# Stationary tiles at the weight ring's 512-byte residue, and two panels whose last units run token tile by token tile

## What is computed

```
x = _layer_norm(DEEPNORM_ALPHA * x + gate1 * y, ln1_g, ln1_b)      # y = merged branches @ w_out
h = x * (1.0 + scale2) + shift2
u = conv3(h @ w_up) + conv_b                                        # 1024 -> 5632, three taps over the tokens
gate, val = split(u);  y = (silu(gate) * val) @ w_down              # 2816 -> 1024
x = _layer_norm(DEEPNORM_ALPHA * x + gate2 * y, ln2_g, ln2_b)       # the output

_layer_norm(x, g, b) = (x - mean(x)) * rsqrt(mean((x - mean(x))**2) + 1e-5) * g + b      # over the 1024 columns
```

## Time and profile before

| | |
|---|---|
| Runs | 1011.33, 1012.34, 1013.93 us; median 1012.34 |
| Profiled execution | 1012.67 us; its span from first to last instruction 1011.1 us |
| Mean granted TensorE clock | 0.985 of 2.4 GHz |
| PE busy | 961.3 us (95%) |
| DVE busy | 747.0 us (74%) |
| ACT busy | 551.7 us (55%) |
| POOL busy | 168.2 us (17%) |
| HBM traffic | 172 GB/s over the span |

### The profile page before, as it was taken

One profiled execution on the slowest core, in us unless ns is written; L12 is line 12 of the kernel. 1 busy time (PEld: TensorE's weight loads), 2 busy tenths in 40 slices (PEclk: granted clock), 3 DMA queues, 4 the chain that ended last, 5 costly groups with the idle time before them and its releaser, 6 DMA issues.

```text
span 1011.1 us, 13813 instructions
## 1 busy us (share of the span) xinstructions
PE 961.3 (95%) x4652; PEld 766.0 (76%) x4652; DVE 747.0 (74%) x1086; ACT 551.7 (55%) x816; POOL 168.2 (17%) x250
## 2 busy tenths in 40 slices
PE   7999999998999899999999999999999699999995
PEld 6787887876767778888888887777777588777884
DVE  5787467876676778886778796756567979999945
ACT  6557646465765455555333436755543367777532
POOL 7000000118100000110111011530000313333400
PEclk9999999998999999999999999999999899999998
DMA  8675443865542347886789564211225255556551
GB/s 259 208 249 156 140 157 123 299 199 172 167 156 88 132 135 243 268 265 213 251 293 316 179 208 148 74 63 50 76 82 189 63 180 168 171 169 215 177 188 41
DMA packets 99746, 175.11 MB, mean 173 GB/s; under 512 B 8252, under 2 KB 36444, under 8 KB 99692
## 3 DMA queue, kind: packets, MB, share of 16 engines
q1 hardware_dynamic: 92460, 148.87, 45.5%
q0 software_dynamic: 7184, 25.50, 7.5%
q10 hardware_dynamic: 48, 0.04, 0.0%
HBM read 173.33 MB, written 1.05 MB: 172 GB/s over the span
## 4 chain that ended last, share of the span: by engine, by line
PE 75%; DVE 13%; ACT 6%; issue 5%; DMA 2%; DVEq 0%; SPq 0%; ACTq 0%
PE acc L706 58%; DVE wlo L1650 3%; PE scores L1108 3%; PE turned L1116 3%; PE turned L758 2%; ACT whi L1233 2%; DVE ltb_lo L1690 1%; DMA raw<-in_w_mem_kv 1%; PE turned L732 1%; DVE turn L1705 1%; PE scores L969 1%; PE scores L902 1%; DVE conv L2385 1%; PE scores L968 1%; DVE turn L1708 1%
## 5 line engine op out<-in xcount | busy, mean ns | idle before, releaser
L1650 DVE TENSOR_TENSOR wlo<-raw,whi 128x1024 fp32r<-128x1024 f32 (+2 forms) x270 | 346.3, 1304 | 111.6 <-ACT whi L1233 103.0
L1233 ACT CAST whi<-raw 128x1024 fp32r<-128x1024 f32 (+2 forms) x270 | 273.5, 1030 | 193.0 <-PE acc L706 148.7
L706 PE MATMUL acc<-whi,lta_lo 128*128 128x512 f32 (+2 forms) x576 | 228.4, 397 | 4.9 <-DVE lta_lo L1690 3.3
L706 PE MATMUL acc<-wlo,lta_hi 128*128 128x512 f32 (+2 forms) x576 | 222.8, 387 | 0.0
L706 PE MATMUL acc<-whi,lta_hi 128*128 128x512 f32 (+2 forms) x576 | 222.5, 386 | 0.0
L706 PEld LDWEIGHTS acc<-whi,lta_lo 128*128 128x128 f32 x576 | 108.6, 189 | 39.5 <-issue 13.5
L706 PEld LDWEIGHTS acc<-wlo,lta_hi 128*128 128x128 f32 x576 | 108.5, 188 | 22.1
L706 PEld LDWEIGHTS acc<-whi,lta_hi 128*128 128x128 f32 x576 | 108.7, 189 | 19.7
L706 PE MATMUL acc<-whi,ltb_lo 128*128 128x512 f32 (+1 forms) x272 | 110.3, 406 | 7.9 <-DVE ltb_lo L1690 4.1
L602 POOL DMA_DIRECT2D wm<-in_w_mod x48 | 34.4, 719 | 466.4 <-DVEq L1750 268.4
L706 PE MATMUL acc<-whi,ltb_hi 128*128 128x512 f32 (+1 forms) x272 | 107.2, 394 | 0.0
(11 more groups left out here) (341 smaller groups left out, 1414.7 us busy)
## 6 DMA issues: line engine op xcount, KB each, us to landing
raw<-in_w_in SPq DMA_DIRECT2D x88, 512.0 KB, 4.1
wm<-in_w_mod POOLq DMA_DIRECT2D x48, 512.0 KB, 5.6
raw<-in_w_up SPq DMA_DIRECT2D x88, 256.0 KB, 3.0
raw<-in_w_up SPq DMA_DIRECT2D x32, 512.0 KB, 4.5
raw<-in_w_down SPq DMA_DIRECT2D x32, 512.0 KB, 4.9
raw<-in_w_down SPq DMA_DIRECT2D x44, 256.0 KB, 3.3
raw<-in_w_mem_kv SPq DMA_DIRECT2D x8, 512.0 KB, 5.8
raw<-in_w_o SPq DMA_DIRECT2D x8, 512.0 KB, 3.4
```

The source lines that it names most:

```text
L706: ins = pe.matmul(acc[s][:, t, 0:n], lhs[part][:, kt0 + kk, tok], w[:, u % RING, kk, 0:n], start=(k == 0 and kk == 0 and j == 0), stop=(la ...
L1233: act.copy(whi[:, s, :, 0:n], raw[:, s, :, 0:n]).then_inc(hi_ready, 1)
L1650: dve.tensor_tensor(wlo[:, s, :, 0:n], raw[:, s, :, 0:n], whi[:, s, :, 0:n].bitcast(F32), ALU.subtract)\
```

## The change

Two parts.

**Addresses.** Tiles are no longer placed by the allocator's scopes but by `Room`, which gives each an address: a multiple of 64 bytes, and, behind `stationary()`, one that is 128 modulo 512. `ckT`, `ltb`, `ff` and `act` (and `arena`, `kvx`, `diag`, the attention's tiles) thus move from 352 to 128 modulo 512, which is what `whi`, `wlo` and `lta` have. `prob`, `probT`, `turn` and `work` move from 160 to 192. `sig` and `tap` take the place behind `ltb`.

**Token order.** `tokens_in_turn` runs the last four units of OUT1 (all it has) and of DN1 (units 7 to 10) first for token tile 0, all four, then for tile 1. The layer norm of tile 0 follows `first_tokens`, that of tile 1 the panel's end. The variance, root, reciprocal and scaling are per tile. ACT's and DVE's splits of UP0.0 to UP0.2 now stand between the two tiles' parts.

```diff
+    LINE, END, TILE, FIRST = 64, 229344, 512, 128
...
+    def stationary(self):
+        return Room(-(-(self.at - self.FIRST) // self.TILE) * self.TILE + self.FIRST)
...
-        one = ExitStack()
+        shared = base.stationary()
+        one = shared.here()
...
-        ltb = [sb(f"ltb_{n}", [P, KT, SEQ], F32R) for n in ("hi", "lo")]
-        kvx = sb("kvx", [P, T, COLS])
-        two = ExitStack()
+        ltb = [sb(f"ltb_{n}", [P, KT, SEQ], F32R, shared) for n in ("hi", "lo")]
+        last = shared.here()
+        kvx = sb("kvx", [P, T, COLS], F32, shared)
+        two = shared.stationary()
...
-                for t in range(T):
+                for t in tokens:
...
-                ins.then_inc(unit_used, 1)
+                if T - 1 in tokens:
+                    ins.then_inc(unit_used, 1)
+                elif last:
+                    ins.then_inc(ev(f"{name}_first_tokens"), 1)
+
+            def tokens_in_turn(name, lhs):
+
+                n = units_of(name)
+                for t in range(T):
+                    for k in range(n - RING, n):
+                        unit(name, k, lhs, tokens=(t,))
...
-            panel("OUT1", lta)
+            tokens_in_turn("OUT1", lta)
...
-            turn_tokens("x3", x, ready="x3_ready")
+            turn_tokens("x3", x, ready="x3_ready", after=2)
...
+            for k in range(FT2 // UNIT - RING):
+                unit("DN1", k, actT)
+            tokens_in_turn("DN1", actT)
...
-            ahead(PLAN.unit["UP0"])
-
-            def variance(name):
+            ahead(PLAN.unit["UP0"] - AHEAD)
+
+            def variance(name, pos):
...
-                sqrt(name, stat[:, 1, 4:6])
-
-            variance("ln1")
+                    act.wait_ge(ev(f"{name}_var"), t + 1)
+                    act.activation(stat[:, 1, 4 + t:5 + t], stat[:, 1, 4 + t:5 + t], ACT.Sqrt).then_inc(ev(f"{name}_std"), 1)
+                    ahead(pos)
+
+            variance("ln1", PLAN.unit["UP0"])
...
+            def layer_norm(gate, name, src, pos, scaled):
+
+                panel_wait(f"{src}0")
...
                 for t in range(T):
-                    ins = dve.tensor_scalar(x[:, t, half], x[:, t, half], stat[:, 1, 2 + t:3 + t], stat[:, 1, 4 + t:5 + t],
-                                            ALU.add, ALU.mult)
-                ins.then_inc(ev("x3_ready"), 1)
+                    residual_sums(gate, src, 0, t)
+                for t in range(T):
+                    if t == 0:
+                        ahead(last_unit(f"{src}1") + 1 - AHEAD)
+                        dve.wait_ge(ev(f"{src}1_first_tokens"), 1)
+                    else:
+                        ahead(pos - 1)
+                        dve.wait_ge(unit_used, RING + last_unit(f"{src}1") + 1)
+                    residual_sums(gate, src, 1, t)
+                    dve.tensor_scalar(stat[:, 1, 2 + t:3 + t], stat[:, 1, 8 + t:9 + t], stat[:, 1, 10 + t:11 + t],
+                                      -1.0 / D, ALU.add, ALU.mult).then_inc(ev(f"{name}_mean"), 1)
+                    dve.wait_ge(ev(f"{name}_mean"), t + 1)
+                    if t == T - 1:
+                        ahead(pos)
+                    scaled(t, lambda: spread_of(name, t))
+
+            def spread_of(name, t):
+
+                v = stat[:, 1, 4 + t:5 + t]
+                dve.wait_ge(ev(f"{name}_sum"), t + 1)
+                var(v, D, LN_EPS).then_inc(ev(f"{name}_var"), 1)
+                dve.wait_ge(ev(f"{name}_std"), t + 1)
+                done(dve.reciprocal(v, v))
+
+            def ln1_scaled(t, spread_known):
+
+                if t == T - 1:
+                    for g in range(2):
+                        b, k = T_USE[f"gate2.{g}"]
+                        dve.wait_ge(t_full[b], k + 1)
+                        dve.tensor_copy(gate_row[:, COLS * g:COLS * g + COLS], tb[b][:]).then_inc(t_free[b], 1)
+                spread_known()
+                for half in (slice(0, COLS), slice(COLS, D)):
+                    dve.tensor_scalar(x[:, t, half], x[:, t, half], stat[:, 1, 2 + t:3 + t], stat[:, 1, 4 + t:5 + t],
+                                      ALU.add, ALU.mult).then_inc(ev("x3_ready"), 1)
...
+            def ln2_scaled(t, spread_known):
+
                 done(dve.scalar_tensor_tensor(work[:, t, :], x[:, t, :], stat[:, 1, 2 + t:3 + t], lnrow[:, 0], ALU.add,
                                               ALU.mult))
-                if t == 0:
-                    layer_norm_var("ln2")
-            inverse("ln2", stat[:, 1, 4:6])
-            for t in range(T):
+                spread_known()
                 dve.scalar_tensor_tensor(x[:, t, :], work[:, t, :], stat[:, 1, 4 + t:5 + t], lnrow[:, 1], ALU.mult, ALU.add)\
                    .then_inc(ev("y_ready"), 1)
```

More of the change, by code:

```diff
@@ L199, with __init__, take, here @@
 LT_ORDER = ["me", "h", "y", "hc", "h2", "x2", "oab", "ym", "x3"]
+class Room:
+    LINE, END, TILE, FIRST = 64, 229344, 512, 128
+    def __init__(self, at):
+        assert at % self.LINE == 0, at
+        self.at = at
+    def take(self, size):
+        self.at += -(-size // self.LINE) * self.LINE
+        assert self.at <= self.END, self.at
+    def here(self):
+        return Room(self.at)
+    def stationary(self):
+        return Room(-(-(self.at - self.FIRST) // self.TILE) * self.TILE + self.FIRST)
 def hybrid_kernel(nc, a, out):
@@ L207, in sem, with sb @@
             return ctx.enter_context(nc.semaphore(name))
-        def sb(name, shape, dt=F32, scope=ctx):
-            return scope.enter_context(nc.sbuf_tensor(name, shape, dt))
+        def sb(name, shape, dt=F32, room=None):
+            room = base if room is None else room
+            v = nc.alloc_sbuf_tensor_at(name, shape, dt, offset=room.at)
+            room.take(int(np.prod(shape[1:])) * (1 if dt is I8 else 4))
+            return v
+        base = Room(16512)
         acc = [ctx.enter_context(nc.psum_tensor(f"acc{i}", [P, T, COLS], F32)) for i in range(2)]
@@ L268, in hybrid_kernel @@
         gmask = sb("gmask", [P, 7, P], I8, one)
-        one.close()
         def ar(at, *shape):
@@ L319, in hybrid_kernel @@
         up = [prob, probT]
-        two.close()
-        diag = sb("diag", [P, KT, P])
-        ones = sb("ones", [P, P])
-        gate_row = sb("gate_row", [P, D])
-        three = ExitStack()
+        later = shared.stationary()
+        diag = sb("diag", [P, KT, P], F32, later)
+        ones = sb("ones", [P, P], F32, later)
+        gate_row = sb("gate_row", [P, D], F32, later)
+        three = later.here()
         qkv = sb("qkv", [P, T, 1536], F32, three)
@@ L331, in hybrid_kernel @@
         ym = work
-        three.close()
-        four = ExitStack()
+        four = later.here()
         lnrow = sb("lnrow", [P, 2, D], F32, four)
@@ L338, in hybrid_kernel @@
         conv = [sb("conv", [P, 4, SEQ], F32, four)[:], work[:, 0].rearrange("p (j s) -> p j s", j=4)]
-        sig = sb("sig", [P, 2, SEQ], F32, four)
-        tap = sb("tap", [P, 4, 4], F32, four)
-        four.close()
+        sig = sb("sig", [P, 2, SEQ], F32, last)
+        tap = sb("tap", [P, 4, 4], F32, last)
         landed = [sem(f"weights_landed{i}") for i in range(RING)]
@@ L690, in _, with unit @@
             pe.sem_inc(unit_used, RING)
-            def unit(name, k, lhs, n=COLS, first_kt=None, i=None, per=0):
+            def unit(name, k, lhs, n=COLS, first_kt=None, i=None, per=0, tokens=range(T)):
                 u, (s, cnt) = PLAN.unit[name] + k, PLAN.bank(name)
@@ L721, in t_begin, with turn_tokens @@
                 return tb[b], t_full[b]
[L723 removed]
+            def turn_tokens(name, src, kts=KT, ready=None, per=2, groups=None, after=0):
                 for g in groups or range(kts // 2):
                     if ready and g % per == 0:
[L727 removed]
+                        pe.wait_ge(ev(ready), after + g // per + 1)
                     bank, full = t_begin(f"{name}.{g}" if kts > 2 else name)
@@ L1209, in _ @@
                             conv_turn(c - 1, i)
-            for c in range(2):
-                for k in range(FT2 // UNIT):
-                    if c == 0 and k == 2:
-                        conv_turn(10)
-                    if c == 0:
-                        pe.wait_ge(conv_mul, k + 1)
-                    unit(f"DN{c}", k, actT)
+            for k in range(FT2 // UNIT):
+                if k == 2:
+                    conv_turn(10)
+                pe.wait_ge(conv_mul, k + 1)
+                unit("DN0", k, actT)
+            for k in range(FT2 // UNIT - RING):
+                unit("DN1", k, actT)
+            tokens_in_turn("DN1", actT)
         def last_unit(name):
@@ L1631, in _ @@
             ahead(PLAN.units)
-            variance("ln2")
+            variance("ln2", PLAN.units)
         @block.vector
@@ L2329, in _, with residual_sums @@
                 lt_dve("ym", lta, groups=(2 * c, 2 * c + 1))
-            def layer_norm_sums(name, src):
+            def residual_sums(gate, src, g, t):
+                part = slice(COLS * g, COLS * g + COLS)
```

(9 more changed lines are left out.)

39 lines of the change are left out of this document (7 added, 32 removed).

## The result

The changed kernel takes 1005.88 us (median of 7 runs, 1001.01 to 1012.32) against 1012.34 (1011.33 to 1013.93): 0.9933 of it, interval 0.991 to 0.9957. It is faster, by 6.5 us (the interval is 4.4 to 9.1) where 7.7 was forecast, inside the range. Its profiled execution took 1008.62 us with a span of 1007.0.

What follows compares the result with a forecast made beforehand. The prediction took PE as 75% of the chain, paying only where PE isn't waiting. It summed -4.85 + 0.4 + 0.45 - 3.73 = -7.7 us against 1012.67, giving 1005.0 us; own range 1002.5 to 1007.8, with rivals 1001.0 to 1009.6.

Steps and rivals of the forecast that it cites:

- The addresses: Matmuls whose stationary tile moves from 352 to 128 modulo 512 get faster, 4.85 us less in all, ends 3.9 and 5.4.
- WD: Its 384 matmuls, all on PE's path, gain 6.1 ns each: 2.3 us less.
- DN and what lies ahead of it: DN's matmuls behind the last convolution, with PE time gained before: 1.65 us less; UP's first part: 0.3 less.
- UP's beat: In UP, DVE, POOL and ACT alone set 12.48 us a panel, so faster matmuls there only lengthen PE's waits: nothing.
- Rival A: The addresses do nothing; slow tiles share being higher in the partition than lta: 1009.8 us, chance 0.12.
- B: UP's pace has a PE step after all, so its ten panels gain 2.8 us: 1002.2 us, chance 0.12.
- C: UP's panels get longer, DVE standing behind one more POOL instruction in each, ten costing 13 us: 1018 us, chance 0.04.
- Token order in OUT1: In OUT1 PE waits 0.3 us for OUT1.3's split and restarts for 0.1: 0.4 us more.
- The first layer norm: Between OUT1 and UP0, splits ahead of tile 1's residual delay the turned x to T + 6.75, T the panel's end: +0.45 us.
- POOL's lock: Behind the first layer norm, POOL's product stretches DVE's subtraction from 0.68 to 4.90 us: neither worse nor better.
- The end: Behind DN1 only one tile's norm remains, 4.98 us where 8.71 was: 3.73 less; second store at most 0.3 less, not counted.
- the clock: A fall to 0.50 of 2.4 GHz for 3.4 us in UP0, behind the layer norm's idle, costs 1.7 us, may come or not.

Runs made afterwards that it cites:

- b1: The changed kernel with ckT, ff, act and ltb at 192 modulo 512, the ring and lta left at 128: 1008.0 us in one execution.
- b2: The changed kernel with everything 224 bytes higher, ring, lta and all other stationary tiles at 352 modulo 512: 1003.35 us in one execution.
- b4: The changed kernel with lta alone moved to 320 modulo 512, all other stationary tiles left at 128: 1011.09 us in one execution.
- e1: The changed kernel with ACT's cast of act_hi in UP behind the next panel's first two weight casts, and ckT 128 bytes on: 1002.81 us.
- e2: Token order with the addresses of before, and ACT's cast of act_hi in UP behind the next panel's first two weight casts: 1008.33 us.
- d2: The changed kernel, POOL's gain and bias behind the last convolution in eight pieces, UP0.1's and UP0.2's splits behind the subtractions, ckT at 320 modulo 512: 995.97 us.
- a2: The token order alone, with the allocator's addresses of before: 1009.32 us against 1012.24 for the kernel before, 0.9974 of it.
- a3: The changed kernel with OUT1 and the first layer norm as before: 1004.16 us against 1012.24 for the kernel before, 0.991 of it.
- a4: The changed kernel run again unaltered, on the chip of the others: 1007.06 us against 1012.24 for the kernel before, 0.9946 of it.
- a1: The new addresses alone, with the old order: 1007.1 us against 1012.24 for the kernel before, 0.9947 of it.

## Why the prediction was right, step by step

- **The addresses, -4.85.** Right in mechanism, and close in size: -5.1 alone by medians, -4.45 by the stages that follow. WD 2.3 forecast, 2.2 measured (97.7 to 95.5). DN and what lies ahead of it 1.95 forecast (1.65, and 0.3 at UP's start); from UP1's first matmul to DN0's 0.5 less, from DN0's to the end of DN1 1.3 less (give or take the wait in DN0): 1.8. UKV 0.3 and 0.3. BA and BB 0.3 and 0.15. UP's beat: nothing, to the hundredth. Rival A had argued from height; b1, b2 and b4 each rule it out. What the prediction drew from the Trainium skill against it ("TensorE: Matmul & The Clock Gate", LDWEIGHTS), that the tiles' places would not matter, does not hold here: the pace is 226.7 or 233.3 ns by the stationary tile's place relative to the moving one's. That it is the load which takes something from the running matmul is the nearest explanation, but no run shows it directly.
- **Rivals B and C.** UP1 to UP10 neither fell by 2.8 nor rose: from UP1's first matmul to DN0's 123.1 us before, 122.6 now. e1 and e2 show what B would have needed: the beat out of the way.
- **Token order in OUT1, +0.4.** 0.32 for the wait at OUT1.3 and 0.11 for the restart behind it (the next matmul starts at 781.30, 0.34 later); from OUT1's first matmul to E it is 10.89 before and 11.38 now, +0.49.
- **The first layer norm, +0.45.** E + 6.86 against E + 6.49: +0.37. By the prediction's mark, T + 6.7 where 6.75 was forecast. Tile 1's residual began at T + 1.4 (forecast 1.5), behind the two splits named. From OUT1's first matmul to UP0's the two terms together are 21.34 to 22.19, +0.85, the forecast's sum.
- **POOL's lock.** It was held to be neither worse nor better: 4.91 and 4.65 us in place of 4.90 and 4.66. Right; that it could be had back, at most the 4.8 us of d2, the prediction didn't ask.
- **The end, -3.73.** 8.71 to 4.96, -3.75, and 0.16 for the store, which was put at nothing, at most 0.3.
- **The sum, -7.7.** In the stages the terms come to -7.5: 0.3 + 2.2 + 0.15 + 0.5 + 1.3 for the addresses, 3.9 for the end, less 0.85. The medians gave -6.5; the stages' sum is well inside their interval, and part of what lies between is the clock. The two profiled executions add up: -7.5, UP0 1.6 less, 4.5 more behind G10 and 0.5 more ahead of UKV make the 4.1 by which the spans differ. The prediction had the clock at 1.7 us in UP0, come or not (before it was 0.50 from 806.72 for 3.41 us; in after's profiled execution that fall didn't come, and UP0 took 1.64 less), and did not think of a fall at 285 us, which came in 4 of the 14 executions profiled here: the changed kernel's, a2's, a3's and b4's, and not in that of before or a4. Why it comes in one execution and not in the next of the same kernel (the changed one and a4) isn't settled. PE had been busy for 8.44 of the 10 us ahead of it in either. Falls of 3.41 us come and go likewise: the one near 337 us is missing in a4 and b2, and one between 614 and 622 us is in a1, a2 and e1 alone. Whether the changed kernel meets them more often than before can't be said either; before's runs spread over 4 us (17 runs), the changed kernel's over 11 (7 runs) and over 6 (a4's 6).
- **What was luck.** That each median lies near its term (5.1 and 2.9, on a chip where both parts together gave 5.2) is partly chance: the clock moves single medians by as much as the terms are worth. The evidence for the sum is in the stages.

## What to carry to other kernels

Compare the starts of matmuls, tile by tile: two paces that differ by 3% for the same shapes can be an address, and giving both operands' tiles the same residue of 256 bytes cost nothing here. But a faster engine pays only where it is the bound, so first find the stage's beat; here one line that loads the sigmoid's table ahead of a loop (3.7 us) and the three moves around the first layer norm (7.0 us) gave more than the addresses and the order together (7.5). And where executions differ by more than the terms in question, read the terms from stages.
